# Expert steps of a hybrid decoder layer: thirteen steps with three shared ones for fourteen with two, and what goes with it

## The reference, cut to what matters

```
g_sel = argmax(softmax(xf @ w_rg + b_rg))            # one of 4 groups
top_w, top_i = top_k(softmax(in_group), 2)           # 2 of its 4 experts
gates = p_group * top_w / sum(top_w), spread over 16 experts
h = silu(xf @ w_g[e]) * (xf @ w_u[e])                # 1024 -> 256
out = sum over e of (h * gates[:, e]) @ w_d[e]       # 256 -> 1024
x = x + g2 * rmsnorm(out, n_post2)
```

## Time and profile before

| | us |
|---|---|
| median of 3 runs | 549.45 (547.32 to 549.88) |
| profiled execution | 548.57 |
| its span | 546.6 |
| PE busy | 522.1 (96%) |
| DVE busy | 259.3 (47%) |
| POOL busy | 155.2 (28%) |
| ACT busy | 151.3 (28%) |
| expert steps on PE | 361.66 to 526.0 |

### The profile page before, as it was taken

The page is one execution under the profiler, slowest core; times in us unless marked ns, Lnnn a source line. Parts: engine busy times, 40 slices in busy tenths (PEclk is TensorE's granted clock), DMA queues, the critical chain, the costliest instruction groups (busy, mean ns, idle before and its releaser), DMA issues.

```text
span 546.6 us, 7575 instructions
## 1 busy us (share of the span) xinstructions
PE 522.1 (96%) x2798; PEld 324.0 (59%) x2798; DVE 259.3 (47%) x759; ACT 151.3 (28%) x293; POOL 155.2 (28%) x166
## 2 busy tenths in 40 slices
PE   8999999999999999999999999788999899899994
PEld 6677755544455454557444445477787777577851
DVE  3443465443033143244453365684776545643347
ACT  7332497711123122132232333400010010000132
POOL 3017000116000000000210020347777747756500
PEclk8999999999999999999999999999999999999998
DMA  9999997899800000009820034879997999996474
GB/s 267 356 328 354 348 321 312 305 387 361 291 0 1 0 0 1 1 4 383 327 78 38 38 116 172 311 278 387 362 362 259 351 396 367 366 377 221 56 196 177
DMA packets 47417, 126.50 MB, mean 231 GB/s; under 512 B 6654, under 2 KB 19358, under 8 KB 41234
## 3 DMA queue, kind: packets, MB, share of 16 engines
q1 hardware_dynamic: 30912, 99.36, 49.6%
q0 software_dynamic: 11408, 22.05, 15.0%
q10 hardware_dynamic: 5058, 4.58, 2.5%
HBM read 116.48 MB, written 17.30 MB: 245 GB/s over the span
## 4 chain that ended last, share of the span: by engine, by line
PE 73%; DMA 10%; DVE 8%; issue 5%; POOL 3%; SPq 1%; ACT 0%; POOLq 0%; ACTq 0%; DVEq 0%
PE psum L811 71%; DMA arena<-gates_dram,slot_tok 5%; DMA ring<-in_w_mod_dram 3%; POOL arena L753 2%; PE psum L814 2%; DMA u_dram<-arena 2%; DVE arena L2378 1%; DVE x L2383 1%; DVE arena L2443 1%; DVE arena L2325 1%; DVE arena L2179 0%; SPq L574 0%; DVE arena L2457 0%; DVE arena L2319 0%; ACT arena L1494 0%
## 5 line engine op out<-in xcount | busy, mean ns | idle before, releaser
L811 PE MATMUL psum<-ring,uT 128*128 128x512 f32 (+1 forms) x384 | 126.5, 522 | 0.0
L811 PEld LDWEIGHTS psum<-ring,uT 128*128 128x128 f32 (+1 forms) x384 | 56.5, 172 | 60.1 <-issue 55.8
L1494 ACT ACTIVATE arena<-psum 128x512 f32<-128x512 f32 (+6 forms) x80 | 35.7, 476 | 164.7 <-PE psum L811 154.0
L811 PE MATMUL psum<-uT,ring 128*128 128x288 f32 x256 | 64.9, 410 | 0.1
L811 PEld LDWEIGHTS psum<-arena,ring 128*128 128x128 f32 x512 | 60.1, 196 | 6.8 <-issue 6.8
L811 PE MATMUL psum<-arena,ring 128*128 128x128 f32 x512 | 60.6, 280 | 3.7 <-DVE arena L2534 2.1
L753 POOL DMA_INDIRECT arena<-u_dram,part_tok x52 | 53.4, 1028 | 21.6 <-issue 14.3
L811 PEld LDWEIGHTS psum<-uT,ring 128*128 128x128 f32 x256 | 47.7, 190 | 16.4 <-issue 4.0
L811 PE MATMUL psum<-ring,arena 128*64 128x256 f32 (+2 forms) x192 | 50.6, 490 | 0.1
L782 POOL DMA_INDIRECT f_dram<-arena,add_tok x26 | 41.6, 1600 | 27.7 <-issue 13.1
L811 PE MATMUL psum<-arena 128*128 128x128 f32 (+6 forms) x253 | 42.3, 330 | 5.4 <-DVE arena L2325 2.4
(11 more groups left out here) (261 smaller groups left out, 603.9 us busy)
## 6 DMA issues: line engine op xcount, KB each, us to landing
ring<-in_w_mod_dram SPq DMA_DIRECT2D x24, 1024.0 KB, 11.9
ring<-in_w_exp_down_dram SPq DMA_DIRECT2D x12, 1024.0 KB, 13.5
ring<-in_w_exp_gate_dram SPq DMA_DIRECT2D x11, 1024.0 KB, 9.7
ring<-in_w_exp_up_dram SPq DMA_DIRECT2D x11, 1024.0 KB, 12.4
ring<-in_w_in_dram SPq DMA_DIRECT2D x10, 1024.0 KB, 10.4
ring<-in_w_out_dram SPq DMA_DIRECT2D x4, 1024.0 KB, 7.0
uT<-in_w_exp_gate_dram SPq DMA_DIRECT2D x4, 1024.0 KB, 13.1
f_dram<-in_consts_dram POOLq DMA_DIRECT2D x2, 1536.0 KB, 16.8
```

Of the source, the lines that this page charges most:

```text
L811: return nc.tensor.matmul(out, lhsT, rhs, start=first, stop=last)
L1494: return nc.scalar.activation(out, src, func, **kw).then_inc(done, 1)
```

## The change

- `FIRST` goes from 3 to 2, and `STEPS` to thirteen steps, of which 4, 7 and 10 are shared. `BIG` becomes 8, `SORTED` 14. Only experts 0 and 1 are loaded early (`early` is cut at 3 × `FIRST`, not at `SLOTS`).
- `f_dram` is one tensor of whole rows; `add_rows` issues one DMA of 1024 columns when both halves of the output are scaled. `s_ost` has two semaphores for four.
- The gates of step e − 1 are gathered at turn e (those of step 0 with those of step 1), into four buffers.
- DVE: `take_input(0)` stands before `numbers(2)`, `new_state(2)` and `(3)` behind the gates; the last step's table is worked out in step 7 (`LAST_AT`).
- PE: `pair_in` waits for the output of the shared step before it, not for the product of the step before; `expert_in` behind a shared step no longer waits for that step's product; `pair_turn` waits for it as a whole.

```
-FIRST = 3
+FIRST = 2
-STEPS = [()] * FIRST + [(0,), (1,), (9, 10), (2,), (3,), (4,), (11, 12), (5,), (6,), (7,), (8,)]
+STEPS = [()] * FIRST + [(0,), (1,), (8, 9), (2,), (3,), (10, 11), (4,), (5,), (12, 13), (6,), (7,)]
+LAST_AT = 7
...
-        early, late = expert_pieces[:SLOTS], expert_pieces[SLOTS:]
+        early, late = expert_pieces[:3 * FIRST], expert_pieces[3 * FIRST:]
...
+        gsl = [tiny(432 + i * NE, NE) for i in range(4)]
...
                     if e >= 2:
-                        pool.wait_ge(s_eoa, e - 1)
-                        pool.wait_ge(s_eod, e - 1)
+                        pool.wait_ge(s_gs[e % 2], 16 * (e // 2))
+                    if e >= 4:
+                        pool.wait_ge(s_eoa, e - 3)
+                        pool.wait_ge(s_eod, e - 3)
...
                 def add_rows(e):
                     pool.wait_ge(s_add, e + 1)
-                    for c in range(2):
-                        pool.wait_ge((s_eoa, s_eod)[c], e + 1)
-                        if e:
-                            pool.wait_ge(s_ost[c][(e - 1) % 2], 16 * ((e - 1) // 2 + 1))
-                        pool.indirect_dma_start(
-                            out=f_dram[c], in_=eo[e % 2][:, c * HALF:(c + 1) * HALF],
...
+                    pool.wait_ge(s_eoa, e + 1)
+                    pool.wait_ge(s_eod, e + 1)
+                    if e:
+                        pool.wait_ge(s_ost[(e - 1) % 2], 16 * ((e - 1) // 2 + 1))
+                    pool.indirect_dma_start(
+                        out=f_dram, in_=eo[e % 2], in_offset=None, compute_op=ALU.add,
...
-                    if 2 <= e < NST + 1:
-                        gather_gates(e - 2)
+                    if e == 2:
+                        gather_gates(0)
+                    if 2 <= e < NST:
+                        gather_gates(e - 1)
...
-                    pe.wait_ge(s_hs, e)
-                    pe.wait_ge(s_hm, FT * e)
+                    earlier = [i for i in range(e) if paired(i)]
+                    if earlier:
+                        pe.wait_ge(s_eoa, earlier[-1] + 1)
+                        pe.wait_ge(s_eod, earlier[-1] + 1)
...
                     if e >= 1:
-                        pe.wait_ge(s_hs, e)
-                        pe.wait_ge(s_hm, FT * e)
+                        done = e - paired(e - 1)
+                        pe.wait_ge(s_hs, done)
+                        pe.wait_ge(s_hm, FT * done)
...
                 orders()
+                take_input(0)
                 numbers(2)
-
-                take_input(0)
-                for h in range(2, NH):
-                    new_state(h)
                 gate_weights()
...
+                for h in range(2, NH):
+                    new_state(h)
...
-                    if e == 2:
+                    if e == LAST_AT:
```

More of the change, by code:

```diff
@@ L201, in build @@
         gates_dram = nc.dram_tensor("gates_dram", (NTOK, NE), F32, kind="Internal").ap()
-        f_dram = [nc.dram_tensor(f"f_dram{c}", (6 * P, HALF), F32, kind="Internal").ap()
-                  for c in range(2)]
+        f_dram = nc.dram_tensor("f_dram", (6 * P, D), F32, kind="Internal").ap()
         psum = ctx.enter_context(nc.psum_tensor("psum", [P, 8 * 512], F32))
@@ L300, in build @@
         rank1 = region(14336 + 3 * TILES * NE, TILES, NE)
-        gsl = [region(14784 + i * NE, NE) for i in range(2)]
         spare = region(14816, 1)
@@ L414, in build @@
         s_eod = sem("s_eod")
-        s_ost = [[sem(f"s_ost{c}{i}") for i in range(2)] for c in range(2)]
+        s_ost = [sem(f"s_ost{i}") for i in range(2)]
         s_add = sem("s_add")
@@ L498, in build @@
         grid = tiny(192, SORTED, SORTED)
-        order = tiny(368, SORTED).bitcast(I32)
-        ordf = tiny(384, SORTED)
+        order = tiny(400, SORTED).bitcast(I32)
+        ordf = tiny(416, SORTED)
         def spread(eng, parts, done):
@@ L768, in gather_gates @@
                     if e >= 2:
-                        pool.wait_ge(s_eoa, e - 1)
-                        pool.wait_ge(s_eod, e - 1)
+                        pool.wait_ge(s_gs[e % 2], 16 * (e // 2))
+                    if e >= 4:
+                        pool.wait_ge(s_eoa, e - 3)
+                        pool.wait_ge(s_eod, e - 3)
                     pool.indirect_dma_start(
-                        out=gsl[e % 2], out_offset=None, in_=gates_dram,
+                        out=gsl[e % 4], out_offset=None, in_=gates_dram,
                         in_offset=bass.IndirectOffsetOnAxis(ap=slot_tok[:, e:e + 1], axis=0))\
@@ L777, in add_rows @@
                     pool.wait_ge(s_add, e + 1)
[L778 to L787 removed]
+                    pool.wait_ge(s_eoa, e + 1)
[4 more added lines that the diff above has]
+                        out=f_dram, in_=eo[e % 2], in_offset=None, compute_op=ALU.add,
+                        out_offset=bass.IndirectOffsetOnAxis(ap=add_tok[:, e:e + 1], axis=0),
+                        bounds_check=NTOK - 1, oob_is_err=False).then_inc(s_ost[e % 2], 16)
                 for e in range(NST + 2):
@@ L1836, in take_out @@
                     if e >= 2:
-                        act.wait_ge(s_ost[0][e % 2], 16 * (e // 2))
+                        act.wait_ge(s_ost[e % 2], 16 * (e // 2))
                     if e < FIRST:
@@ L2499, in pick_gates @@
                                              float(at + 1), None, ALU.is_equal))
-                    link(v.tensor_tensor(out=masked[:, 0], in0=gsl[e % 2][:, FIRST:NE], in1=mine,
+                    link(v.tensor_tensor(out=masked[:, 0], in0=gsl[e % 4][:, FIRST:NE], in1=mine,
                                          op=ALU.mult))
```

20 lines of the change are left out of this document (11 added, 9 removed).

## The result

The changed kernel takes 552.8 us (median of 5, 551.9 to 554.7) where the kernel before took 548.4 in the same runs: ratio 1.0075, 95% interval 1.0042 to 1.0107. The forecast was 543.6. The profiled execution took 554.7 us, the longest of the five, its span 552.6; before, 548.57 and 546.6.

The account below looks back on a forecast made before the run. PE was taken as the bound, with full DMA engines right behind. Stage −5.7, end +1.0 and store wait −0.3 made −5.0 us against 548.57: 543.6; 8 in 10 from 531 to a little above 551, the forecast's own 539 to 549.

Parts of the forecast that it names:

- DVE's wait for gates: Sign: with gates gathered a step sooner, DVE's waits for them, 26.4 us before, would be near 0.
- the software queue holds under 22%: Sign: from merged additions, the software queue's share of DMA time would fall below 22%, from 22.4%.
- the 1.99 us wait before the second half of step 0: Sign: at the start, `new_state` behind the gates would make PE wait a new 2.0 us.
- The merge saving: DMA engines in the loading stretch: whole-row additions give back 4.0 us, a third of the software queue's 12.1 us excess.
- Rival 1: DMA engines: bytes bind, not packets, so merging gives 0 and the kernel takes 547.6 us; chance 0.13.
- the 136.5 of the step with no saving at all: Weight loads: 38 pieces behind the order take 136.5 us before any merge saving, 139.7 less a 3.2 us hole.
- The start of the order: SP's first late weight load: the order is known 0.65 us later, so loading starts at 360.65 us.
- The stops themselves: PE's waits for weights in the expert stage: 2.7 us at step 8 and 8.8 us at step 11.
- The clock behind a stop: PE after the stop at step 11: the granted clock falls to 0.50, costing 1.7 us.
- The tail: Behind the expert stage: the last additions stand in line, first read after 8.3 us instead of 7.3, costing 1.0 us.
- 13 of PE's 18.9 us: Expert stage: PE alone gains 18.9 us, of which 13 turn into waits for weights, leaving 5.7.
- Rival 3: Additions' single chain: decides from landings of 12.0 us on; at 13.3 the kernel takes 558 us; chance 0.12.

Follow-up runs that it names:

- e2: The changed kernel, with only half of each late down-projection piece loaded, work on the other engines the same: 535.8 us, ratio 0.9750 to the kernel before.
- e3: The changed kernel with the additions of before (two tensors, two chains of half rows): 551.0 us, ratio 1.0031 to the kernel before.
- e8: The changed kernel with its shared steps at 3, 6 and 9 instead of 4, 7 and 10: 549.0 us, ratio 1.0016 to the kernel before.
- e5: The changed kernel with the fourteen steps and three early experts of before, and additions in half rows: 540.2 us, ratio 0.9862 to the kernel before.
- e1: The changed kernel with nine early weight pieces, as before, instead of six: 551.1 us, ratio 1.0017 to the kernel before.
- e11: The kernel before with four gate buffers, gates a step sooner and the change's DVE order at the start: 542.4 us, ratio 0.9866.

## Why the prediction was wrong

**The order of the bounds was right.** PE alone gains much (e2: the kernel is 17 us faster once the loads are lighter), the loads bind at steps 8 and 11, the clock falls to 0.50 behind both stops, DVE's wait for gates shrinks to one of 3.8 us, the software queue holds under 22%, and the 1.99 us wait before the second half of step 0 is there. Each was named as a sign, and each came.

**The steps that failed are two terms of the sum**: merging the additions was to bring the weights 4.0 us sooner and brought at most 1.2, and the end was to cost 1.0 us and cost 5.5. With two smaller terms, the start and the clock, they make up the miss: the stage's end misses by 6.2 us (526.49 for 520.3) and the tail by 4.5, together 10.7 of the 11.1 between forecast and profiled execution.

- **The merge saving, 4.0 us, is mis-sized: at most 1.2.** It was a third of the excess time of the software queue's packets. The queue's time did fall, by 2.4 us, but the mean rate did not rise (365 and 366 GB/s), and the weights came no sooner. The 38 pieces took 136.9 us, which is the 136.5 of the step with no saving at all. The failing inference is "time on a queue given back is given to the next queue". Rival 1 said that the bytes bind, and priced this term rightly, though not the whole (547.6); that it is the bytes isn't shown. The Trainium skill ("DMA: Bandwidth & Descriptors", Specifications) gives a core's memory limit as about 358 GB/s. The trace doesn't bear it out as a hard limit: the mean of the full stretch was 366, with 399 from 460 to 480 us. The Trainium skill's rule to coalesce (same page, Rules for kernel authors), which the prediction set against it, names 64 KB as the size under which a transfer is mostly overhead; an addition of half rows moves 128 rows of 2 KB, 256 KB in all.
- **The start of the order, 1.0 us.** The first late piece went out at 361.65, forecast 360.65. In e3, with the same program ahead of it, it went out at 360.57: this is scatter between executions and no error of a step. Together the two make 5.3 us: 498.5 for 493.2. The stops themselves were forecast as 2.7 and 8.8 us and were 6.4 and 5.0 (with the 1.2 at step 7, 12.6 for 11.5): piece 26 came at 457.5 for 451.3, since the first pieces took more than their share of the time. That the sum comes near is partly luck; only the landing of piece 38 set the stage's end.
- **The clock behind a stop, 1.7 us for one step.** After stops of 6.42 and 4.96 us, 32 products took 6.2 us and not 3.7, so each stop costs 2.5 us. Of the first nothing is seen, since the loads bind again behind it; the second makes 0.8 us.
- **The tail, 1.0 us, was 5.5.** The step gave 8.3 us from step 12's start to the first read (its parts, 5.5 + 5 − 2.4, make 8.1); it is 11.3 (515.82 to 527.13). The pair's addition was issued 1.7 us before step 11's end and not 2.4, landed after 5.8, the last one went out 0.8 later and landed after 6.3. I had taken "about 5", the landing of a 2 KB half, for a row of twice the bytes. With halves the same stretch is 8.05 us (515.37 to 523.42), the 8.3 of the forecast. The rest of the tail (1.6 us) was not in the sum: PE waits for DVE, which waited 4.8 us for the late reads (a stop of 3.24 us on PE; 0.44 in e3, 0.28 in e8), and the first pair of products behind it takes 2.08 us at the lower clock for 1.13 before.

**The largest omission was no single term.** The forecast took the change as one. It saw that 13 of PE's 18.9 us would turn into waits for weights, but did not ask what the same change would do with fourteen steps. Fourteen steps with the gates, the waits and the order (e5) are 7.6 us faster than before, and the thirteen steps on top of that cost 9.3 us.

What the rows show of why: step 11 of the thirteen begins with the same two pieces of the 48, the 43rd and the 44th, as step 12 of the fourteen. The 44th lands at 491.5 in e5, at 497.1 in e1 and at 498.5 in the changed kernel, and PE was there at 484.32 in e2, where no load held it. Behind it come 21.6 us of PE's work in e5 (494.87 to 516.51), and 25.4 and the lower clock with thirteen. So the loads deliver that piece later, PE wants it sooner, and has more to do behind it. Three pieces more behind the order at 3.6 us each would be 11 us, near the 9.3 to 9.7 us lost, but that likeness is no proof: e1 takes the three away and gets back 3.

**Rival 3** (the additions' chain) was wrong in its place and right in kind: PE waited for no addition in the loading stretch, though they land in 10.3 us there (below its 12.0) and POOL did wait for landings, but the end of the same chain took 3 us.

What isn't settled: whether the bytes or the packets of the loads bind, since no run changed one without the other; the thirteen steps with a larger ring, or with all pairs early, were not tried, nor `LAST_AT` alone. Of e5's gain over e11 the ratios tell 0.2 us, the medians, from two chips, 2.1.

**The version that beats both** is e5: 540.2 us, 0.9862 (0.9833 to 0.9891) of the kernel before and about 2% under the changed one. It takes the gates a step sooner, the order at the start, the looser waits and the later table of the last expert, and leaves out the thirteen steps and the whole rows.

## What to carry to other kernels

Before a step is taken out of a loop whose weights come from memory, count what has to land before each of its steps, at the pace the trace shows per piece: a queue 15 us ahead of the engine is already the bound of the next version. Price a change with several parts part by part, since one of them may carry more than the sum. And follow a wait on DVE back to what DVE itself waited for: late gathers stood behind most of two kinds of wait that looked unrelated.

## What the runs showed of the hardware

- An addition of 4 KB rows lands in 10.3 us beside the loads and 5.8 to 6.3 without them (changed kernel); one of 2 KB rows in 9.7 and 4.4 to 4.8 (e3; 9.4 and 4.9 before). Twice the bytes cost 0.6 us under load and some 1.4 without. But two halves overlap each other, and the whole row waits for the whole row before it.
- A quarter fewer packets on the software queue left the mean rate of a full stretch where it was: 365 (e3) and 366 GB/s.
- The length of a wait doesn't by itself tell whether the clock falls behind it: before the second half of step 0, 32 products took 3.84 us behind 1.98 us of idle in e3, and 5.47 us behind 1.98 us in e8, with the same program ahead of both.
